# A hybrid encoder layer on one core: the projections change from three products of rounded halves to one fp32 product

## The reference

```python
def reference(x, p, ...):
    h = x
    h = h + token_mixers(rmsnorm(h, norm_mix), w_in, ...)        # 6168 input columns, GLA and mLSTM heads, w_out
    h = h + peer_ffn(rmsnorm(h, norm_ffn), peer_query, sub_keys, peer_u, peer_v)
    gate = sigmoid(rmsnorm(h, norm_ple) @ w_ple_gate)
    h = h + gate * (p @ w_ple)
    return rmsnorm(h, norm_final)
```

```python
    a = gelu(einsum('thkd,td->thk', expert_u[idx], xb))
    return einsum('thk,thkd->td', softmax(top_s) * a, expert_v[idx])
```

## Time and profile before

| | us |
|---|---|
| median of 3 runs | 1990.37 (1986.71 to 1992.75) |
| profiled execution, its span | 1990.1 |
| PE busy | 1587.0 |
| DVE busy | 1122.1 |
| POOL busy | 923.5 |
| ACT busy | 436.1 |
| matmuls of the projections (L1296, L1309), busy | about 1056 (records overlap) |
| DVE's 96 subtractions of weights (L754) | 219.8 |
| ACT's 96 rounding copies (L455) | 183.6 |

### The profile page before, as it was taken

The page is one execution under the profiler, slowest core; times in us unless marked ns, Lnnn a source line. Parts: engine busy times, 40 slices in busy tenths (PEclk is TensorE's granted clock), DMA queues, the critical chain, the costliest instruction groups (busy, mean ns, idle before and its releaser), DMA issues.

```text
span 1990.1 us, 17044 instructions
## 1 busy us (share of the span) xinstructions
PE 1587.0 (80%) x5668; PEld 934.4 (47%) x5671; DVE 1122.1 (56%) x1533; ACT 436.1 (22%) x581; POOL 923.5 (46%) x1142
## 2 busy tenths in 40 slices
PE   6999999999567777777777777776776776689896
PEld 5998888889552223222222222322222222233475
DVE  4567646566784646646456465564655646442445
ACT  3445345334210111111101011010110101111253
POOL 0000000000577676586675866758667687573200
PEclk9999999999879999999999999999999999999998
DMA  6445535655689999999999999999999999998852
GB/s 204 158 152 169 169 127 181 220 170 169 254 316 422 396 423 402 421 405 398 423 399 408 417 405 422 398 399 420 402 422 403 402 422 386 423 421 330 315 169 85
DMA packets 130331, 648.25 MB, mean 326 GB/s; under 512 B 14124, under 2 KB 14232, under 8 KB 63720
## 3 DMA queue, kind: packets, MB, share of 16 engines
q0 software_dynamic: 74496, 541.36, 66.5%
q1 hardware_dynamic: 51408, 105.91, 15.9%
q10 hardware_dynamic: 4376, 0.29, 0.2%
HBM read 645.42 MB, written 2.10 MB: 325 GB/s over the span
## 4 chain that ended last, share of the span: by engine, by line
POOL 32%; PE 30%; issue 20%; DMA 9%; DVE 5%; ACT 1%; DVEq 1%; ACTq 1%; POOLq 0%
PE acc L1296 17%; POOL u_ring L404 11%; POOL v_ring L416 9%; POOL tick L415 7%; DMA v_ring<-in_peer_v_dram,idxv 6%; PE acc L1309 5%; POOL tick L403 5%; PE acc L1513 3%; DMA u_ring<-in_peer_u_dram,idxu 3%; DVE w_lo L754 1%; DVE u_ring L1120 1%; PE mix L1352 1%; ACT w_hi L455 1%; PE mix L1513 1%; PE mix L1362 0%
## 5 line engine op out<-in xcount | busy, mean ns | idle before, releaser
L1120 DVE CUSTOM_DVE_ANT_0 u_ring<-u_ring,xn 128x2048 f32<-128x2048 f32 x256 | 583.5, 2292 | 525.5 <-DMA u_ring<-in_peer_u_dram,idxu 525.2
L1513 PE MATMUL mix<-v_ring,diag 128*128 128x512 f32 x1024 | 487.3, 621 | 171.5 <-DMA v_ring<-in_peer_v_dram,idxv 169.6
L1513 PE MATMUL acc<-v_ring,diag 128*128 128x512 f32 x992 | 459.0, 609 | 156.0 <-DMA v_ring<-in_peer_v_dram,idxv 153.7
L1513 PEld LDWEIGHTS mix<-v_ring,diag 128*128 128x128 f32 x1024 | 191.1, 196 | 467.8 <-issue 249.3
L1513 PEld LDWEIGHTS acc<-v_ring,diag 128*128 128x128 f32 x992 | 182.4, 192 | 430.3 <-issue 257.1
L754 DVE TENSOR_TENSOR w_lo<-raw,w_hi 128x2048 fp32r<-128x2048 f32 x96 | 219.8, 2291 | 199.8 <-ACT w_hi L455 198.7
L404 POOL DMA_INDIRECT u_ring<-in_peer_u_dram,idxu x256 | 310.5, 1213 | 40.3 <-issue 32.4
L416 POOL DMA_INDIRECT v_ring<-in_peer_v_dram,idxv x256 | 273.0, 1067 | 39.0 <-issue 16.2
L636 ACT ACTIVATE diag<-ident,wgt 128x128 f32<-128x128 f32 x240 | 92.8, 399 | 880.0 <-PE mix L1513 470.1
L415 POOL TENSOR_TENSOR tick<-tick 128x1 f32<-128x1 f32 x256 | 176.2, 688 | 202.6 <-PE acc L1513 108.5
L455 ACT ACTIVATE w_hi<-raw 128x2048 fp32r<-128x2048 f32 x96 | 183.6, 1913 | 324.5 <-PE acc L1296 195.0
(11 more groups left out here) (255 smaller groups left out, 1048.3 us busy)
## 6 DMA issues: line engine op xcount, KB each, us to landing
raw<-in_w_in_dram SPq DMA_DIRECT2D x48, 1024.0 KB, 5.1
raw<-in_w_out_dram SPq DMA_DIRECT2D x16, 1024.0 KB, 5.2
raw<-in_peer_query_dram SPq DMA_DIRECT2D x16, 1024.0 KB, 5.3
raw<-in_w_ple_gate_dram SPq DMA_DIRECT2D x16, 1024.0 KB, 5.1
u_ring<-in_peer_u_dram,idxu POOLq DMA_INDIRECT x256, 15.2
v_ring<-in_peer_v_dram,idxv POOLq DMA_INDIRECT x256, 14.8
h<-in_x_dram SPq DMA_DIRECT2D x2, 1024.0 KB, 6.8
wple<-in_w_ple_dram POOLq DMA_DIRECT2D x1, 2048.0 KB, 18.0
```

The source lines that it names most:

```text
L1120: V.tensor_tensor_reduce(out=u_ring[:, k % DEEP, :], in0=u_ring[:, k % DEEP, :], in1=xn2[:, b, :], scale=1.0, scalar=0.0, op0=ALU.mult, op ...
L1513: ins = T.matmul(pairs[j // 2][:, (j % 2) * CW:(j % 2 + 1) * CW], diag[:, k % DEEP, :], v_ring[:, k % DEEP, j * CW:(j + 1) * CW], start=Fa ...
```

## The change

The halves go. Tokens are kept once, in fp32, in two tiles used in turn: `t_even` (stages A and Q) and `t_odd` (B and G), written by `t_scale` itself, which signals `t_done`. `split_hi`, `split_lo`, `t_hi_part` and `t_lo_part` are removed from ACT and DVE with all their calls. PE reads the loaded slice from `raw` and does one fp32 matmul where there were three: 16 in a column slice, 8 in a token slice, 16 in the small products. `raw` has eight slots of 8 KB per partition; SP may load slice s when PE has used slice s - 8. `v_ring` now shares memory with slots 4 to 7. All four slices of chunk 20 are loaded in stage Q, then the row of `norm_final`; the slices from 84 on wait for `peer_ready` and for the last `v` rows of DVE. SP's loops are written out.

```diff
-        t_hi = next_to("t_hi", [P, KT, S], F32R)
-        t_lo = next_to("t_lo", [P, KT, S], F32R)
-        v_ring = at("v_ring", [P, DEEP, D], F32, base + 16 * KB)
-        raw = next_to("raw", [P, NQ, KQ, CW], F32)
-        w_hi = next_to("w_hi", [P, 2, KQ, CW], F32R)
-        w_lo = next_to("w_lo", [P, 2, KQ, CW], F32R)
+        t_even = next_to("t_even", [P, KT, S], F32)
+        t_odd = next_to("t_odd", [P, KT, S], F32)
+        v_ring = at("v_ring", [P, DEEP, D], F32, used[0] + NQ * 8 * KB)
+        raw = next_to("raw", [P, 2 * NQ, KQ, CW], F32)
...
+        def t_of(phase):
+            return t_even if phase in "AQ" else t_odd
...
+        def await_slice(eng, s):
+            eng.wait_ge(raw_in[s % (2 * NQ)], 16 * (s // (2 * NQ) + 1))
...
+                def load(s, src):
+                    if s >= 2 * NQ:
+                        sp.wait_ge(slice_used, s - 2 * NQ + 1)
+                    sp.dma_start(raw[:, s % (2 * NQ), :, :], src).then_inc(raw_in[s % (2 * NQ)], 16)
+
                 def stream(w, g0, n, col0):
                     quarter = slices(w)
...
+                    for c in range(n):
                         for q in range(NQ):
...
+                            load((g0 + c) * NQ + q, quarter[q][:, :, col0 + c * CW:col0 + (c + 1) * CW])
...
-                quarter = slices(w_ple_gate[0])
-                for q in range(NQ):
-                    if q == NQ // 2:
-                        sp.wait_ge(v_in[DEEP - 1], 16 * (TOPK // DEEP) * G)
-                    sp.wait_ge(lo_done, (gG - 1) * NQ + q + 1)
-                    sp.dma_start(raw[:, q, :, :], quarter[q][:, :, 0:CW]).then_inc(raw_in[q], 16)
+                stream(w_ple_gate[0], gG, 1, 0)
 
                 sp.wait_ge(xn2_ready, NB)
                 sp.dma_start(nrow[:, :], norm_final.partition_broadcast(P)).then_inc(nfin_in, 16)
+                sp.wait_ge(peer_ready, NB)
+                sp.wait_ge(v_free_dve, len(dve_picks))
                 stream(w_ple_gate[0], gG + 1, ND - 1, CW)
...
-                def split_hi(s):
-                    g, q = s // NQ, s % NQ
-                    act.wait_ge(raw_in[q], 16 * (g + 1))
-                    if s >= 2:
-                        act.wait_ge(slice_used, s - 1)
-                    act.activation(w_hi[:, s % 2, :, :], raw[:, q, :, :], ACT.Copy).then_inc(hi_done, 1)
...
-                    dst = staged(phase, i)
+                    dst = part(phase, i)
...
-                def split_lo(s):
-                    q = s % NQ
-                    dve.wait_ge(hi_done, s + 1)
-                    if s >= 2:
-                        dve.wait_ge(slice_used, s - 1)
-                    V.tensor_tensor(w_lo[:, s % 2, :, :], raw[:, q, :, :], w_hi[:, s % 2, :, :].bitcast(F32),
-                                    ALU.subtract).then_inc(lo_done, 1)
...
+                    s = g * NQ + q
+                    await_slice(pe, s)
                     for k in range(KQ):
                         kt = q * KQ + k
                         for b in blocks:
...
-                            for n, (a, w) in enumerate(((t_hi, w_hi), (t_hi, w_lo), (t_lo, w_hi))):
-                                ins = T.matmul(acc[set_no][:, b * CW:(b + 1) * CW], a[:, kt, tok], w[:, s_slot, k, :],
-                                               start=(kt == 0 and n == 0), stop=(kt == KT - 1 and n == 2))
+                            ins = T.matmul(acc[g % 2][:, b * CW:(b + 1) * CW], t_of(phase)[:, kt, b * P:(b + 1) * P],
+                                           raw[:, s % (2 * NQ), k, :], start=(kt == 0), stop=(kt == KT - 1))
...
-                            for n, (w, a) in enumerate(((w_hi, t_hi), (w_hi, t_lo), (w_lo, t_hi))):
-                                ins = T.matmul(acc[set_no][:, c * S:(c + 1) * S], w[:, s_slot, k, c * P:(c + 1) * P], a[:, kt, :],
-                                               start=(kt == 0 and n == 0 and c % 2 == 0), stop=(kt == KT - 1 and n == 2),
-                                               skip_group_check=True)
+                            ins = T.matmul(acc[g % 2][:, c * S:(c + 1) * S], raw[:, s % (2 * NQ), k, c * P:(c + 1) * P],
+                                           t_of(phase)[:, kt, :], start=(kt == 0 and c % 2 == 0), stop=(kt == KT - 1),
+                                           skip_group_check=True)
...
-                        T.matmul(m[0:2 * NSM, 0:S], wsm_hl[:, kt, :], t_hi[:, kt, :], start=(kt == 0), stop=False, skip_group_check=True)
-                        ins = T.matmul(m[0:NSM, 0:S], wsm_hl[:, kt, 0:NSM], t_lo[:, kt, :], start=False, stop=(kt == KT - 1), skip_group_check=True)
+                        ins = T.matmul(m[0:NSM, 0:S], wsm[:, kt, :], t_even[:, kt, :], start=(kt == 0), stop=(kt == KT - 1))
```

More of the change, by code:

```diff
@@ L198, in build @@
         keys_in, nffn_in, nfin_in, p_in, wple_in = (sem(n) for n in ("keys_in", "nffn_in", "nfin_in", "p_in", "wple_in"))
-        raw_in = [sem(f"raw_in{q}") for q in range(NQ)]
-        hi_done, lo_done, slice_used = sem("hi_done"), sem("lo_done"), sem("slice_used")
+        raw_in = [sem(f"raw_in{q}") for q in range(2 * NQ)]
+        slice_used = sem("slice_used")
         acc_free = [sem(f"acc_free{i}") for i in range(2)]
@@ L263, in item, with part @@
             return (i % 2, i // 2) if phase in "AB" else (i // 2, i % 2)
-        small_t = y[0:2 * NSM, 0, 0:S]
+        small_t = y[0:NSM, 0, 0:S]
         def src_blocks(phase):
             return {"A": h, "B": y, "G": h}[phase]
-        def part(t, phase, i):
+        def t_of(phase):
+            return t_even if phase in "AQ" else t_odd
+        def part(phase, i):
+            t = t_of(phase)
             if phase == "Q":
@@ L300, in _ @@
                 sp.wait_ge(wsm_in, 32)
+                def load(s, src):
+                    if s >= 2 * NQ:
+                        sp.wait_ge(slice_used, s - 2 * NQ + 1)
+                    sp.dma_start(raw[:, s % (2 * NQ), :, :], src).then_inc(raw_in[s % (2 * NQ)], 16)
                 def stream(w, g0, n, col0):
                     quarter = slices(w)
-                    def chunk(g, col):
+                    for c in range(n):
                         for q in range(NQ):
[L307 to L316, removed]
+                            load((g0 + c) * NQ + q, quarter[q][:, :, col0 + c * CW:col0 + (c + 1) * CW])
                 stream(w_in[0], 0, 2, 0)
@@ L591, in _ @@
                         act_slot(g * NQ + q)
-                split_hi(NQ * gB)
                 put_out(NA - 1)
[L594 to L598, removed]
-                    if s in (NQ * gQ - 2, NQ * gQ - 1):
-                        t_hi_part("Q", (s - NQ * gQ + 2,))
-                split_hi(NQ * gQ)
-                t_hi_part("Q", (2,))
-                split_hi(NQ * gQ + 1)
-                t_hi_part("Q", (3,))
                 for g in range(gQ, gG):
                     for q in range(NQ):
-                        if g * NQ + q >= NQ * gQ + 2:
-                            split_hi(g * NQ + q)
                         if (g, q) == (gQ, 2):
@@ L1293, in token_slice, with column_slice @@
                         for b in blocks:
-                            tok = slice(b * P, (b + 1) * P)
-                            for n, (a, w) in enumerate(((t_hi, w_hi), (t_hi, w_lo), (t_lo, w_hi))):
-                                ins = T.matmul(acc[set_no][:, b * CW:(b + 1) * CW], a[:, kt, tok], w[:, s_slot, k, :],
-                                               start=(kt == 0 and n == 0), stop=(kt == KT - 1 and n == 2))
+                            ins = T.matmul(acc[g % 2][:, b * CW:(b + 1) * CW], t_of(phase)[:, kt, b * P:(b + 1) * P],
+                                           raw[:, s % (2 * NQ), k, :], start=(kt == 0), stop=(kt == KT - 1))
                     if blocks[-1] == NB - 1:
                         ins.then_inc(slice_used, 1)
-                def column_slice(set_no, s_slot, q, lo_count):
-                    pe.wait_ge(lo_done, lo_count)
+                def column_slice(phase, g, q):
+                    s = g * NQ + q
+                    await_slice(pe, s)
                     for k in range(KQ):
@@ L1375, in pe_slot @@
                         m = mix_of("smt")
-                        T.matmul(m[0:RANK, 0:S], sm_sum[:, 0:RANK], small_t, start=True, stop=True)
-                        T.matmul(m[0:H, S:2 * S], sm_sum[:, RANK:RANK + H], small_t, start=True, stop=True)
-                        T.matmul(m[0:H, 2 * S:3 * S], sm_sum[:, RANK + H:NSM], small_t, start=True, stop=True).then_inc(mix_ready, 1)
+                        T.matmul(m[0:RANK, 0:S], ident[0:NSM, 0:RANK], small_t, start=True, stop=True)
+                        T.matmul(m[0:H, S:2 * S], ident[0:NSM, RANK:RANK + H], small_t, start=True, stop=True)
+                        T.matmul(m[0:H, 2 * S:3 * S], ident[0:NSM, RANK + H:NSM], small_t, start=True, stop=True).then_inc(mix_ready, 1)
                     if s == 5:
@@ L1456, in after_b @@
                     if r == 1:
```

(14 more changed lines are left out.)

108 lines of the change are left out of this document (17 added, 91 removed).

## The result

The changed kernel takes 2080.20 us in the median of 4 runs (2075.54 to 2081.62), the kernel before 1988.54 beside it (4 runs, 1982.90 to 1992.75). The ratio is 1.0464, 95% interval 1.0437 to 1.0490: slower by 4.6%, where 2088 with a range of 2068 to 2110 was forecast.

The account below looks back on a forecast made before the run. PE was taken to bound the projection and gate stages, a chain through scores, top-k and gathers the query stage, gathers the expert stage. +86.5 - 3 + 14 = +97.5 us on 1990.1 gave 2088 us, range 2068 to 2110.

Parts of the forecast that it names:

- The price per slice: Projection slices on PE: 6.92 us each in fp32, a token slice 1.46 us longer, a column slice 1.16 us.
- rival 1: Projection slices on PE: fp32 costs four full passes, four rounded products a slice, total 2123 us; chance 0.10.
- rival 2: Projection slices on PE: fp32 costs no more than the three products, making the kernel faster, 1970 us; chance 0.05.
- Start: Before the first projection matmul: no wait for the split, only transposes left in front, -3.1 us.
- A and B: Projection stages, PE-bound: +18.6 column slices, +70.1 token slices, +3.2 small products, -2.3 waits; with the start, +86.5 us.
- The query stage: Between projections and experts: later first scores +6.7 us, removed subtractions and waits give back more; -3 us, bounds -15 and +5.
- POOL's wait: End of the query stage: POOL's 4.58 us wait for the last query slice goes, because PE is done earlier.
- rival 4: Query stage: with DVE rid of 16 subtractions and POOL issuing beside it, shrinks up to 15 to 20 us; chance 0.12.
- Expert stage: The gather-bound stage after the queries: change 0, since the number of gathers and their ring depth stay.
- Gate stage: Last projection stage, PE-bound: +12.9 us from longer slices, +1 for half clock, thus +14 us; loads hidden.
- rival 3: Projections: dense fp32 loses two to four hundredths of PE clock, total 2100 to 2110 us; chance 0.13.
- The sum: Whole kernel: +86.5 - 3 + 14 = +97.5 us on the profiled span of 1990.1 us, giving 2088 us.

Follow-up runs that it names:

- The three runs with other prices and the same structure: Changed kernel with each fp32 matmul of a projection slice replaced by three, four or one bf16 matmuls: 1947.85, 2107.31 and 1657.73 us.
- the second profile: The kernel before, with no edit, executed and profiled once more: 1984.94 us.
- the run with the extra subtractions: Changed kernel with four of eight slots in use, plus a DVE subtraction for each query-stage slice but the first two: 2092.99 us.
- The last two runs: Kernel before with only the query stage in fp32: 1980.35 us; with only that stage's last eight slices in fp32, POOL re-adding token halves: 1971.87 us.

## Why the prediction was right

**The price per slice: right.** 6.92 was forecast for both kinds, 6.91 and 6.87 were measured. The three runs with other prices and the same structure move the time with it, and give rival 1 and rival 2 their answers: fp32 is cheaper than four separate matmuls and dearer than three. In A, B and G nearly all else that was taken away was work that nobody waited for; over the whole kernel it was 234.5 us of DVE and 196.5 of ACT. The known exceptions are the small terms of the sum: the start, 2.3 us of waits for `w_lo`, and the waits for `t_lo` in the gate stage.

**Start: right.** The first projection matmul is at 26.06 (forecast 26.19).

**A and B: 8 us too long, mostly through one silent assumption.** Forecast was a start of the query stage at 527.5, measured 519.9. The token price explains 48 x 0.05 = 2.4. The rest is in the kernel before, not in the change: its first profile lost 5.6 us more to half-clock stretches in A and B than its second, and the kernel after, at 1.00, lost little to them. Against the second profile A and B grew by 494.0 - 406.4 = 87.6 us, where the terms without the start make 18.6 + 70.1 + 3.2 - 2.3 = 89.6, or 87.2 with the measured token price. The step that was off is the silent one, that the time of a stretch of the profiled execution carries over; the terms of the sum were right within 2.4 us.

**The query stage: the mechanism right, the gain mis-sized.** Forecast -3 (-15 to +5), measured -9.3. By starts in the two timelines, in us, where the changes add up to -9.4:

| piece of the stage | before | after | change | forecast |
|---|---|---|---|---|
| first slice to first scores | 42.4 | 49.2 | +6.8 | +6.7 |
| to the first gather of `u` | 19.1 | 15.1 | -4.0 | -2.2 |
| to the first product | 10.1 | 6.4 | -3.7 | none |
| first to last product | 63.9 | 59.5 | -4.4 | -4.4, perhaps -10 |
| to the first gather of `v` | 4.2 | 0.0 | -4.1 | -4.6, POOL's wait |

The forecast's own terms make -4.5, and -3 was taken. What they left out is 5.5 us around POOL's first issue. Two subtractions follow the index list, and the sum had them nowhere; they are not on DVE's own path, but POOL ran beside them. Before:

```profile
500.04 4.49 DVE L754 TENSOR_TENSOR w_lo<-raw,w_hi 128x2048 fp32r<-128x2048 f32 x2 [0.19 <-issue]
500.13 2.25 POOL L403 TENSOR_TENSOR tick<-tick 128x1 f32<-128x1 f32 x1
502.54 2.90 POOL L404 DMA_INDIRECT u_ring<-in_peer_u_dram,idxu  x1 [0.16 <-issue]
```

After, with DVE idle:

```profile
583.71 0.19 POOL L390 TENSOR_TENSOR tick<-tick 128x1 f32<-128x1 f32 x1
584.06 1.03 POOL L391 DMA_INDIRECT u_ring<-in_peer_u_dram,idxu  x1 [0.15 <-issue]
```

The step and the issue were 3.9 us longer beside the subtractions, and the run with the extra subtractions brings the long steps back. The rest, under 2 us, is a later landing of the first gather and stays open. In all, eight subtractions stood between the first scores and the last product, not the three that the sum counts. The five among the products make 11 us of DVE, of which 4.4 came back; DVE waits for gathers there. None of the eight shows a wait of more than 0.2 us. The last two runs show the whole stage in parts: fp32 here and nowhere else is worth 7.8 us, and giving back the late first scores another 8.5. Of rival 4, the part about POOL's issues beside a quieter DVE came; the products did not close up beyond the sure 4.4, and the gain is about half of its 15 to 20.

**Expert stage: 0 forecast, 2.8 measured** in the stretch of the `v` gathers, within what the other runs scatter (1280.8 to 1286.5).

**Gate stage: right.** Forecast +14, measured 122.7 - 111.4 = 11.3 from the last gather, or 1945.17 to 2058.43 against 1873.85 to 1974.79, +12.3, from the end of PE's part of the experts' sum; against the second profile of before it is 13.3 from the last gather. PE did not wait for slice 84 or any later one.

**The clock (rival 3): did not come.** Dense fp32 over 494 us was granted 1.00, and the later stages 0.95 to 0.98. With four slots and the extra subtraction the same stretch had 0.99 and took 495.7 us, against 492.3 and 494.0 in the other two.

**The sum.** Spans differ by 83.6 us, medians by 91.7, and the forecast was 97.5. The profiled execution of before was a long one for its kernel and that of after the shortest of four: against the second profile of before the spans differ by 90.6. What is left of the excess, 6.9, is 6.1 in the query stage, 2.0 in A and B and 0.8 at the start, less 2.5 in the `v` gathers and with 0.5 behind them. The errors nearly all have one sign, so the forecast does not owe its place in the range to terms that cancel.

## What to carry to other kernels

Replacing several cheap matmuls by one dear one is decided by the price of the whole set on PE, read at two shapes from rows that the kernel already has, and by which stage has PE as its bound: here fp32 at 3.8 times a short matmul loses to three of them in three stages and wins in the fourth. Relieving an engine is worth nothing in a stage that it does not bound. It can be worth more than its own time on the path where another engine's instructions get long beside it: here POOL's step of 0.19 us took 2.25. A net figure can also hide two terms of opposite sign, as the query stage's 9.3 us hid 6.8 and 16.1. So a change of this kind should be tried stage by stage, and the forecast should be made from more than one execution, since the same code can differ by 5 us in one stage through the clock alone.

## What the runs showed of the hardware

The rounded fp32 type was not at the speed of bf16: 0.120 against 0.1133 us at 256 columns and 0.2275 against 0.225 at 512. An fp32 matmul cost 0.859 us and 0.432, which is 3.8 bf16 matmuls at both sizes. The four passes that the Trainium skill states ("FP8 and Floating Point Precision", TensorE Precision Notes) are neither confirmed nor refuted by this: if an instruction is p for each pass and o once, 4p + o = 0.859 and p + o = 0.225 give p = 0.211 and o = 0.014 us, but two prices always fit two unknowns, and at 256 columns o comes out as 0.007, so it would not be a constant of the instruction. What the runs do show is that the rule must not be multiplied with the price of a whole instruction, as I had done for rival 1: four bf16 matmuls in a row cost 0.900.

Small POOL instructions got long beside long DVE ones. A step of 128x1 that takes 0.19 us took 2.25 and 2.31 beside subtractions of 128x2048, and an issue of a gather 2.90 instead of 1.03. The 2.25 us step ended at 502.38, about when the first of the two subtractions did (two in 4.49 us from 500.04), and the issue 0.9 us after the second. The products have the same effect: beside the one from 637.72 to 640.05 in the kernel after an issue took 2.82 us. What holds POOL there no run shows.

With the same work on PE, the length of stages A and B took two values in the traces, 412.0 and 411.9 us in two executions and 406.4 in two others, by whether PE was granted the half clock for some stretches. What decides it in an execution was not found.
